# Gathering experts' tokens from unscaled rows, and a fourth staged piece of weights in the tile this frees

## The chip, the cores and the metric

The kernel runs on one core of a Trainium2 chip. The metric is the device time of one execution, in microseconds (us). Before the change it is 1026.22 us, the median of three runs (1024.59, 1026.22 and 1026.88 us).

## The reference

Two transformer blocks for 256 tokens of width 1024, all in float32. The change touches the end of the first block, a mixture of experts whose router picks, for each token, one of 4 groups and then 2 of its 8 experts:

```
xf = _rmsnorm(h, norm_g).reshape(t, d)          # h * rsqrt(mean(h*h) + eps) * norm_g
...                                             # group and expert logits, top 2, gates
def expert_block(args):
    xb, e = args                                # rows of xf that chose expert e
    hid = jax.nn.silu(xb @ w_gate[e]) * (xb @ w_up[e])
    return hid @ w_down[e]
...
y = jnp.zeros((t, d), out.dtype).at[token_of].add(out)   # out is scaled by the gate
h = h + y
```

Each of the 32 experts has three matrices of 2 MB (gate, up, down), so that 192 MB are read once. Every number that the experts see is a row of `h` times one factor per row (the rsqrt) times one gain per channel (`norm_g`, called `norm_ffn` in the kernel).

## The kernel before

Before the experts the kernel runs dense layers on TensorE (PE), each block of weights loaded by SyncE's queue (SP), rounded by ScalarE (ACT) and completed by VectorE (DVE). The last two dense blocks are `co1` and `xv2`; `xv2` is computed in quarters, and between them PE computes the router's logits from the turned rows `h2T`.

The experts run in 8 quads of four. For one quad PE first **gathers**: `gather` multiplies the normed rows (`normed`, as the stationary operand, 8 chunks of 128 channels by 2 tiles of tokens) with `sel3`, a matrix of ones and zeros that `select_slots` on DVE makes, so that each of the four experts gets up to 32 columns. ACT (`gathered_low`) and DVE (`gathered_high`) move the result out of PSUM into `xgT`. Then six weight units follow, of four pieces each (one per expert): u = 0 and 1 are the halves of gate, 2 and 3 those of up, 4 and 5 those of down. The first four are consumed in line 2875, the last two in line 2894. `scatter` brings the outputs back to token order, scaled by the gates, and DVE's `add_outputs` adds them to `h`. In the next quad the gather comes before the scatter of the quad before it.

The order of the loads is written out by hand in SP's program. A unit occupies one of four buffers (`weight_unit`), and a load waits until PE has used what lies there: `moe.unit_used` counts used units, `moe.first_used` the first halves of u = 0 and u = 1. For the first quad much is loaded ahead, while the dense layers still run, into tiles that happen to be free. Three of the four pieces of its unit u = 4 (the first half of down) are **staged** in such tiles: piece 0 in part of `main` and `squares`, piece 2 in `y_slots` and `wide_gain`, piece 1 in `mem2T`. When PE has used buffer 0, ACT copies them there (`place_staged`). The fourth piece has no tile and is loaded straight into buffer 0 after PE has used it, in two halves (line 728). Behind it, line 733 loads u = 5 (four pieces, 4 MB) in eight halves into buffer 1, each group of four once PE has used the first or the second half of u = 1. `load_quad` goes on with the second quad.

`wide_gain` holds `norm_ffn` broadcast to all partitions until DVE has normed the rows (`norm_tokens`); only then SP loads the second half of piece 2 into it (line 671). The tile `normed` takes junk of ACT's squares and then the normed rows, and these are read by all 8 gathers. Channels are stored there by chunks (`by_chunk`): the channel 8p + k of a row lies at position 128k + p, since the experts' weights are read with channel 8p + k in partition p.

Of the kernel before, what the change touches and what calls it, by code (L numbers as in the profile page):

```python
# [27 lines left out]
ALU = mybir.AluOpType  # L28
# [3 lines left out]
P = 128  # L32
T = 256
TT = T // P
# [28 lines left out]
EXTRA_PARTS = ((0, 4, 0, 4), (1, 8, 0, 4))  # L63
# [101 lines left out]
SCALED_ROWS = ["h2", "h3"]  # L165
# [52 lines left out]
def build(nc, A, out):  # L218
    with ExitStack() as ctx:
# [21 lines left out]
        def as_f32(x):  # L241
# [23 lines left out]
        wide_gain = sb("wide_gain", [P, D])  # L265
        lam_s = sb("lam_s", [P, 8])
# [111 lines left out]
                  [y_slots, wide_gain[:, :]]]  # L378
# [66 lines left out]
        staged_landed = [sem(f"staged_piece_landed{i}") for i in range(3)]  # L445
# [153 lines left out]
        def _(sp):  # L599
# [23 lines left out]
            for t in range(TT):  # L623
# [4 lines left out]
                      (wide_gain[:, :], A["norm_ffn"].broadcast_to([P, D])),  # L628
# [35 lines left out]
            def load_staged(i, halves=range(2)):  # L664

                if i == 1:
                    whole = mem2T.rearrange("p (k n) -> p k n", k=FC // 2)
                    sp.dma_start(whole, down_w_of[i, :, 0:2, :]).then_inc(staged_landed[i], 16)
                else:
                    for k in halves:  # L670
                        sp.dma_start(staged[i][k], down_w_of[i, :, k, :]).then_inc(staged_landed[i], 16)

            for name in FIRST_BLOCKS[2:]:
# [8 lines left out]
                elif name == "co0":  # L682
# [3 lines left out]
                    load_unit(2, (2,), up_w_of, 0, at=2)  # L686
                    sp.wait_ge(head_summed, len(HEAD_SQUARES))
# [24 lines left out]
            for half in range(2):  # L712
                for q in range(2):
# [116 lines left out]
        def _(act):  # L830
# [338 lines left out]
            square_rows("h2", h, normed, "co")  # L1169
# [54 lines left out]

            act_quad(0, first=True)
            act.wait_ge(params_landed, 16 * N_PARAMS)
# [156 lines left out]
        def _(dve):  # L1383
# [504 lines left out]

            def by_chunk(x):

                return x.rearrange("p (c q) -> p q c", c=KC)

# [5 lines left out]
            def norm_tokens(t):  # L1898

                v.scalar_tensor_tensor(by_chunk(normed[:, t, :]), h[:, t, :].rearrange("p (q c) -> p q c", c=KC),  # L1900
                                       rstd[:, row0 + t:row0 + t + 1],
                                       wide_gain[:, :].rearrange("p (q c) -> p q c", c=KC),
                                       ALU.mult, ALU.mult).then_inc(normed_ready, 1)

            norm_tokens(0)
            split_lo("xv2", [1])
            norm_tokens(1)

# [104 lines left out]
            def gathered_high(S, n):  # L2013
                dve.wait_ge(S.gathered, n + 1)
                v.tensor_copy(xgT[:, 512:1024], bank[1][:, :]).then_inc(S.hi_drained, 1)

            def add_outputs(S, n, between=None):
# [15 lines left out]
            def dve_quad(S, n, following, between=None):  # L2033
# [9 lines left out]
                add_outputs(S, n, between)  # L2043
# [7 lines left out]
            with dve.Fori(0, 2 * LAST_PAIR) as i:  # L2051
# [18 lines left out]
            for p in range(2):  # L2070
                gathered_high(moe, last_quad + p)
# [1176 lines left out]
```

## Time and profile before

| | |
|---|---|
| profiled execution, its own time | 1026.24 us |
| its span in the trace | 1024.5 us |
| median of three runs | 1026.22 us |
| PE busy | 856.6 us (84%) |
| DVE busy | 458.7 us (45%) |
| ACT busy | 332.9 us (32%) |
| read from memory | 293.40 MB, 287 GB/s over the span |

The span is the time between the first and the last recorded instruction; the execution's own time is 1.74 us longer. The page cuts the span into 40 slices of 25.6 us. PE is at nine tenths in the dense parts, and at five to seven tenths from slice 12 to slice 28, where the experts are; there the DMA engines are at nine tenths throughout.

### The profile page before, as it was taken

What the parts mean: (1) busy time and instruction counts of PE and PEld (TensorE: products, weight loads), DVE (VectorE), ACT (ScalarE), POOL (GpSimd) and SP (SyncE); (2) the same over time, 40 slices, a digit from 0 to 9 for tenths busy, and PEclk for the clock granted to TensorE, in tenths of its full rate; (3) what the DMA queues carried; (4) which work ended last, traced back from release to release, by engine and by line L of the source; (5) the groups of instructions that cost most, each with busy time, mean ns of one, the idle gap of its engine ahead of it and who ended that gap; (6) DMA issues with size and microseconds to landing.
All of it is one profiled execution on the core that took longest, in us unless ns stands there. A gap on an engine that the chain in (4) does not pass through costs nothing.

```text
span 1024.5 us, 13523 instructions
## 1 busy us (share of the span) xinstructions
PE 856.6 (84%) x5437; PEld 593.4 (58%) x5437; DVE 458.7 (45%) x859; ACT 332.9 (32%) x534; POOL 23.2 (2%) x35
## 2 busy tenths in 40 slices
PE   8998999999994566767566666656999999999997
PEld 8877888798631131313112131312788899999995
DVE  4778676574621020201102021010876788656695
ACT  5656654764320000000001000000534555455532
POOL 1030010100000000000000000000000000000000
PEclk9999999999998897878869788888999999999999
DMA  9743466587999999999999999999555354444541
GB/s 324 263 165 104 154 230 234 177 335 267 357 402 423 420 422 421 422 421 420 423 421 422 422 421 420 422 421 404 186 189 180 124 165 133 156 151 138 185 143 44
DMA packets 76287, 295.29 MB, mean 288 GB/s; under 512 B 6754, under 2 KB 7236, under 8 KB 53828
## 3 DMA queue, kind: packets, MB, share of 16 engines
q1 hardware_dynamic: 73876, 291.37, 73.9%
q10 hardware_dynamic: 2352, 3.10, 0.9%
q8 instruction: 41, 0.67, 0.3%
q14 instruction: 18, 0.15, 0.0%
HBM read 293.40 MB, written 1.05 MB: 287 GB/s over the span
## 4 chain that ended last, share of the span: by engine, by line
PE 58%; DMA 17%; SPq 14%; DVE 6%; ACT 2%; issue 2%; POOL 0%; POOLq 0%; ACTq 0%; DVEq 0%
DMA ring<-in_w_e_down 16%; PE bank L2448 12%; SPq L644 11%; PE bank L2450 11%; PE bank L2449 11%; PE bank L2894 4%; PE bank L2875 3%; PE bank L2850 3%; SPq L659 2%; PE bank L2382 2%; PE bank L2926 2%; DVE ring_rounded L1445 2%; ACT ring_rounded L907 1%; DMA ring<-in_w_in 1%; PE bank L2979 1%
## 5 line engine op out<-in xcount | busy, mean ns | idle before, releaser
L1445 DVE TENSOR_TENSOR ring_rounded<-ring,ring_rounded 128x2048 fp32r<-128x2048 f32 x79 | 181.0, 2291 | 120.4 <-ACT ring_rounded L907 120.0
L907 ACT ACTIVATE ring_rounded<-ring 128x2048 fp32r<-128x2048 f32 x79 | 151.3, 1915 | 170.3 <-PE bank L2450 157.1
L2875 PE MATMUL bank<-ring,main 128*32 128x512 f32 x768 | 116.6, 762 | 75.1 <-DMA ring<-in_w_e_up 53.4
L2449 PE MATMUL bank<-ring_rounded 128*128 128x256 f32 (+1 forms) x456 | 143.5, 315 | 0.0
L2450 PE MATMUL bank<-ring_rounded 128*128 128x512 f32 x320 | 124.9, 390 | 0.0
L2875 PEld LDWEIGHTS bank<-ring,main 128*32 128x32 f32 x768 | 28.3, 135 | 154.2 <-issue 87.5
L2025 DVE TENSOR_TENSOR h<-bank,h 128x512 f32<-128x512 f32 x32 | 22.0, 690 | 166.0 <-PE bank L2926 166.0
L2894 PE MATMUL bank<-ring,main 128*32 128x512 f32 x384 | 61.0, 789 | 39.9 <-DMA ring<-in_w_e_down 39.2
L2448 PE MATMUL bank<-uT_rounded,ring_rounded 128*128 128x256 f32 x320 | 92.7, 290 | 0.0
L2450 PE MATMUL bank<-uT_rounded,ring_rounded 128*128 128x256 f32 x320 | 90.5, 283 | 0.0
L2449 PEld LDWEIGHTS bank<-ring_rounded 128*128 128x128 f32 x456 | 86.9, 191 | 5.0
L2448 PE MATMUL bank<-ring_rounded,uT_rounded 128*128 128x512 f32 x208 | 82.7, 398 | 1.7 <-ACT main L1265 0.8
L2449 PE MATMUL bank<-ring_rounded,uT_rounded 128*128 128x512 f32 x208 | 81.1, 390 | 0.0
L2010 DVE SCALAR_TENSOR_TENSOR main<-main,bank 128x512 f32<-128x512 f32 x8 | 5.5, 687 | 140.2 <-PE bank L2875 140.2
L2450 PEld LDWEIGHTS bank<-ring_rounded 128*128 128x128 f32 x320 | 60.1, 188 | 12.9
L2894 PEld LDWEIGHTS bank<-ring,main 128*32 128x32 f32 x384 | 14.1, 137 | 83.2 <-DMA ring<-in_w_e_down 48.7
L2448 PEld LDWEIGHTS bank<-uT_rounded,ring_rounded 128*128 128x128 f32 x320 | 61.3, 192 | 1.7 <-issue 1.4
L2450 PEld LDWEIGHTS bank<-uT_rounded,ring_rounded 128*128 128x128 f32 x320 | 61.3, 192 | 0.0
L1188 ACT ACTIVATE main<-bank 128x512 f32<-128x512 f32 x8 | 4.8, 597 | 158.2 <-PE bank L2382 158.2
L2448 PE MATMUL bank<-ring_rounded 128*128 128x512 f32 x136 | 54.2, 398 | 1.5 <-DVE ring_rounded L1431 0.9
L1196 ACT ACTIVATE main<-bank 128x512 f32<-128x512 f32 x16 | 9.6, 597 | 123.5 <-PE bank L2894 123.5
L2448 PEld LDWEIGHTS bank<-ring_rounded,uT_rounded 128*128 128x128 f32 x208 | 39.1, 188 | 11.8 <-issue 2.1
(334 smaller groups left out, 1333.8 us busy)
## 6 DMA issues: line engine op xcount, KB each, us to landing
ring<-in_w_in SPq DMA_DIRECT2D x46, 1024.0 KB, 5.1
ring<-in_w_e_gate SPq DMA_DIRECT2D x44, 1024.0 KB, 25.9
ring<-in_w_e_up SPq DMA_DIRECT2D x44, 1024.0 KB, 26.2
ring<-in_w_e_down SPq DMA_DIRECT2D x36, 1024.0 KB, 25.9
main<-in_w_e_down SPq DMA_DIRECT2D x13, 1024.0 KB, 26.6
main<-in_w_e_up SPq DMA_DIRECT2D x12, 1024.0 KB, 26.9
main<-in_w_e_gate SPq DMA_DIRECT2D x12, 1024.0 KB, 26.4
ring<-in_w_ckv SPq DMA_DIRECT2D x8, 1024.0 KB, 5.0
```

Of the source, the lines that this page charges most:

```text
L644: sp.dma_start(weight_unit(b, at + i, chunks), w_of[e, :, h * n:(h + 1) * n, :])\
L659: sp.dma_start(weight_unit(unit_buffer(p, u), i, chunks)[:, k:k + 1, at], w_of[e, :, 2 + k:3 + k, at]).then_inc(last_landed[n], 16)
L907: a.activation(rounded(hi_half(name, h)), raw_half(name, h), ACT.Copy).then_inc(hi_made, 1)
L1445: v.tensor_tensor(rounded(raw), raw, as_f32(hi_half(name, h)), ALU.subtract).then_inc(split_made, 1)
L2025: v.tensor_tensor(hs, b[:, :], hs, ALU.add).then_inc(S.added, 1)
L2382: return nc.tensor.transpose(dst, src, ident[0:k, 0:k])
L2448: mm(dst, left[0], right[0], start=first, stop=False, skip_group_check=True)
L2449: mm(dst, left[0], right[1], start=False, stop=False, skip_group_check=True)
L2450: last = mm(dst, left[1], right[0], start=False, stop=last_one, skip_group_check=True)
L2850: last = mm(dst, normed[:, t, k * P:(k + 1) * P], sel3[:, t, :], start=t == 0, stop=t == TT - 1)
L2875: last = mm(bank[2 + part][on, :], xg3[:, h * (KC // 2) + k, on], weight_unit(unit_buffer(p, u), e, KC)[:, k, :], start=h + k == 0, stop=h ...
L2894: ins = mm(bank[4 + half][on, :], hidT3[:, c, on], weight_unit(unit_buffer(p, u), e, FC)[:, k, half * 512:half * 512 + 512], start=c == 0, ...
```

## The change

- PE gathers from `h` itself, not from `normed`. The chunk of channels is picked by the access pattern: 128 channels at a distance of 8 floats (32 bytes) instead of 128 adjacent ones. The gather now comes before any sum is added to `h`.
- The row factor goes into the selection: `select_slots` multiplies the ones by `rstd`. The channel gain is applied where `xgT` is filled: ACT's one copy of 512 columns becomes four of 128 with a scale, DVE's copy becomes a multiplication by the broadcast gain. `norm_tokens` is gone, and with it PE's and SP's waits for it. The gain is loaded as 128 x 8 (`expert_gain`) instead of 128 x 1024.
- The experts' sums go to `normed`: the first quad is copied there, quads 1 to 5 are added there, quads 6 and 7 go to `h` as before, and behind the gather of quad 7 DVE adds `normed` to `h` (2 instructions of 128x1024).
- `normed` is thereby free while the first block's last dense layers run, and takes the fourth piece of u = 4. It is loaded with the second half of piece 2 ahead of `load_staged(0)`; both halves of line 728 are gone, and ACT places four pieces. ACT's junk of the squares of `h2` goes to `main` and `xv2`.

```diff
-EXTRA_PARTS = ((0, 4, 0, 4), (1, 8, 0, 4))
+EXTRA_PARTS = ((0, 4, 0, 4), (0, 8, 0, 4))
...
-                  [y_slots, wide_gain[:, :]]]
+                  [y_slots, wide_gain[:, :]], [normed[:, 0, :], normed[:, 1, :]]]
...
-                      (wide_gain[:, :], A["norm_ffn"].broadcast_to([P, D])),
+                      (expert_gain[:, :], A["norm_ffn"][0].rearrange("(p k) -> p k", p=P)),
...
                     load_unit(2, (2,), up_w_of, 0, at=2)
+                    load_staged(3)
+                    load_staged(2, [1])
                     sp.wait_ge(head_summed, len(HEAD_SQUARES))
                     load_staged(0)
...
                         load_unit(2, (GROUP - 1,), up_w_of, 0, at=GROUP - 1)
-                        sp.wait_ge(normed_ready, 2 * SCALED_ROWS.index("h2") + 2)
-                        load_staged(2, [1])
             load_staged(1)
-            for k, used in enumerate((moe.first_used, moe.unit_used)):
-                sp.wait_ge(used, 1)
-                sp.dma_start(weight_unit(0, GROUP - 1, FC)[:, k:k + 1, :], down_w_of[GROUP - 1, :, k:k + 1, :])\
-                    .then_inc(unit_landed[0], 16)
...
-            square_rows("h2", h, normed, "co")
+            for t in range(TT):
+                wait_drained(act, f"co0_{t}")
+                wait_drained(act, f"co1_{t}")
+                at = NORM_AT["h2"][1] + t
+                ins = a.activation((main[:, 0:D], xv2)[t], h[:, t, :], ACT.Square, accum_out=mean_sq[:, at:at + 1])
+            ins.then_inc(row_squared, 1)
...
-                a.activation(xgT[:, 0:512], bank[0][:, :], ACT.Copy).then_inc(S.lo_drained, 1)
+                for k in range(KC // 2):
+                    ins = a.activation(xgT[:, k * P:(k + 1) * P], bank[0][:, k * P:(k + 1) * P], ACT.Copy,
+                                       scale=expert_gain[:, k:k + 1])
+                ins.then_inc(S.lo_drained, 1)
...
-                for i, parts_ in ((0, 2), (2, 2), (1, 1)):
+                for i, parts_ in ((0, 2), (2, 2), (3, 1), (1, 1)):
...
-            norm_tokens(0)
             split_lo("xv2", [1])
-            norm_tokens(1)
...
-                        last = v.tensor_scalar(select[:, lo:lo + CAP], slot_no[:, :], rank_flat[:, col], None,
-                                               ALU.is_equal)
+                        last = v.tensor_scalar(select[:, lo:lo + CAP], slot_no[:, :], rank_flat[:, col],
+                                               rstd[:, row0 + t:row0 + t + 1], ALU.is_equal, ALU.mult)
...
-                        hs = h[:, t, half * 512:half * 512 + 512]
-                        v.tensor_tensor(hs, b[:, :], hs, ALU.add).then_inc(S.added, 1)
+                        at = slice(half * 512, half * 512 + 512)
+                        if into == "new sums":
+                            ins = v.tensor_copy(normed[:, t, at], b[:, :])
+                        else:
+                            to = (normed if into == "sums" else h)[:, t, at]
+                            ins = v.tensor_tensor(to, b[:, :], to, ALU.add)
+                        ins.then_inc(S.added, 1)
...
+            gathered_high(moe, last_quad + 1)
+            dve.wait_ge(moe.added, last_quad * 4 + 8)
+            for t in range(TT):
+                ins = v.tensor_tensor(h[:, t, :], normed[:, t, :], h[:, t, :], ALU.add)
+            link(ins)
...
-                        last = mm(dst, normed[:, t, k * P:(k + 1) * P], sel3[:, t, :], start=t == 0,
-                                  stop=t == TT - 1)
+                        last = mm(dst, h[:, t, :].rearrange("p (q c) -> p c q", c=KC)[:, k, :], sel3[:, t, :],
+                                  start=t == 0, stop=t == TT - 1)
...
-            pe.wait_ge(normed_ready, 2 * SCALED_ROWS.index("h2") + 2)
```

SP's queue, before, around the early loads behind the dense block `co0` (line 616 loads dense blocks, 644 whole pieces of expert units, 671 halves of staged pieces; the semaphore that a load waits for stands in brackets):

```order
L616 DMA ring<-in_w_co 128x4x512 [waits bank_filled1]
L644 DMA ring<-in_w_e_gate 128x2048 [waits bank_filled1]
L644 DMA main<-in_w_e_up 128x2048 [waits row_squared]
L671 DMA main<-in_w_e_down 128x1024 [waits head_summed]
L671 DMA squares<-in_w_e_down 128x1024
L644 DMA main<-in_w_e_up 128x2048 [waits bank_filled7]
L644 DMA ring<-in_w_e_gate 128x2048 [waits bank_filled3]
```

The same place in SP's queue now:

```order
L617 DMA ring<-in_w_co 128x4x512 [waits bank_filled1]
L645 DMA ring<-in_w_e_gate 128x2048 [waits bank_filled1]
L645 DMA main<-in_w_e_up 128x2048 [waits row_squared]
L669 DMA normed<-in_w_e_down 128x2048
L672 DMA wide_gain<-in_w_e_down 128x1024
L672 DMA main<-in_w_e_down 128x1024 [waits head_summed]
L672 DMA squares<-in_w_e_down 128x1024
L645 DMA main<-in_w_e_up 128x2048 [waits bank_filled7]
L645 DMA ring<-in_w_e_gate 128x2048 [waits bank_filled3]
```

Two loads, 1 MB into `normed` and 0.5 MB into `wide_gain`, have moved in here, without a wait of their own.

SP's queue, before, from the last piece that is loaded ahead into the first loads that wait for the first quad (`moe_half_of_first_unit_used` is `moe.first_used`, `moe_weight_unit_used` is `moe.unit_used`):

```order
L668 DMA main<-in_w_e_down 128x2048
L728 DMA ring<-in_w_e_down 128x1024 [waits moe_half_of_first_unit_used]
L728 DMA ring<-in_w_e_down 128x1024 [waits moe_weight_unit_used]
L733 DMA ring<-in_w_e_down 128x1024 [waits moe_half_of_first_unit_used]
L733 DMA ring<-in_w_e_down 128x1024 x3
L733 DMA ring<-in_w_e_down 128x1024 [waits moe_weight_unit_used]
L733 DMA ring<-in_w_e_down 128x1024 x3
L644 DMA main<-in_w_e_gate 128x2048 [waits moe_weight_unit_used]
```

And now:

```order
L669 DMA main<-in_w_e_down 128x2048
L730 DMA ring<-in_w_e_down 128x1024 [waits moe_half_of_first_unit_used]
L730 DMA ring<-in_w_e_down 128x1024 x3
L730 DMA ring<-in_w_e_down 128x1024 [waits moe_weight_unit_used]
L730 DMA ring<-in_w_e_down 128x1024 x3
L645 DMA main<-in_w_e_gate 128x2048 [waits moe_weight_unit_used]
```

The two halves of line 728 are gone, so that nothing stands between the last piece loaded ahead and the eight halves of u = 5, whose first waits as before for the second count of `moe.first_used`.

## Rows read from the trace of the kernel before

**Rows 1.** The page's part 2: what the DMA engines moved, in 40 slices.

```profile
GB/s 324 263 165 104 154 230 234 177 335 267 357 402 423 420 422 421 422 421 420 423 421 422 422 421 420 422 421 404 186 189 180 124 165 133 156 151 138 185 143 44
```

**Rows 2.** Engines by stretch: length, busy us and instructions, PE's clock, DMA share, GB/s.

```profile
203.00:224.00 21.00, 21.00 (x148) 20.00 (x147) 15.74 (x36) 14.86 (x33) 1.31 (x1) 1.00 1.00 397
...
228.00:231.00 3.00, 3.00 (x15) 2.59 (x14) 0.78 (x2) 1.28 (x4) 0.00 (x0) 1.00 0.00 0
...
281.00:285.00 4.00, 4.00 (x40) 1.17 (x36) 0.22 (x1) 3.75 (x6) 0.00 (x0) 1.00 0.89 309
...
540.00:600.00 60.00, 38.63 (x244) 13.34 (x241) 7.83 (x24) 3.96 (x7) 0.00 (x0) 0.86 1.01 421
```

**Rows 3.** Timeline of SP's queue: start, length of issuing, line, what is loaded.

```profile
202.42 0.59 SPq L671 DMA_DIRECT2D main<-in_w_e_down  x1
...
216.04 6.92 SPq L616 DMA_DIRECT2D ring<-in_w_co  x2
...
262.68 0.43 SPq L671 DMA_DIRECT2D wide_gain<-in_w_e_down  x1
...
275.39 2.04 SPq L728 DMA_DIRECT2D ring<-in_w_e_down  x2
279.33 4.86 SPq L733 DMA_DIRECT2D ring<-in_w_e_down  x8
```

**Rows 4.** Loads issued at 216.04, 230.37, 277.10 and 279.33: size, us to landing.

```profile
ring<-in_w_co SPq DMA_DIRECT2D x1, 1024.0 KB, 8.8
...
ring<-in_w_e_gate SPq DMA_DIRECT2D x1, 1024.0 KB, 4.9
...
ring<-in_w_e_down SPq DMA_DIRECT2D x1, 512.0 KB, 5.5
...
ring<-in_w_e_down SPq DMA_DIRECT2D x1, 512.0 KB, 4.6
```

**Rows 5.** Timeline of PE in the first quad: gather, then unit u = 0.

```profile
269.74 3.73 PE L2850 MATMUL bank<-main,normed 128*128 128x128 f32 x32
273.40 3.64 PE L2875 MATMUL bank<-ring,main 128*32 128x512 f32 x32
```

**Rows 6.** Weight loads (ns min/median/max): gather, hidden at 288, probabilities at 224.

```profile
L2850 PEld LDWEIGHTS bank<-main,normed x32: 188/192/193, 269.5 to 273.1; 128*128 128x128 f32 x32
...
L2382 PEld LDWEIGHTS bank<-ident,main x4: 198/209/223, 288.7 to 289.0; 128*128 128x128 f32 x4
...
L2382 PEld LDWEIGHTS bank<-ident,main x4: 140/141/144, 223.9 to 224.3; 128*128 128x128 f32 x4
```

**Rows 7.** Chain of waits, four transposes each: hidden at 288, rotated keys at 804.

```profile
288.66 0.75 PE bank L2382 x4
...
804.82 0.66 PE bank L2382 x4
```

**Rows 8.** Timeline of DVE around the router and the first selection.

```profile
260.24 2.03 DVE L1900 SCALAR_TENSOR_TENSOR normed<-h,rstd,wide_gain 128x1024 f32<-128x1024 f32 x1
262.31 0.42 DVE L1924 SCALAR_TENSOR_TENSOR main<-bank,rstd,b_router 128x36 f32<-128x36 f32 x2
...
267.34 1.26 DVE L1990 TENSOR_SCALAR main<-slot_no,rank 128x32 f32<-128x32 f32 x8
...
270.22 1.74 DVE L1999 TENSOR_SCALAR main<-slot_no,rank,gates 128x32 f32<-128x32 f32 x8
```

**Rows 9.** Timeline of ACT: 128-column copies, split of `co1`, first gather's copy, staged pieces.

```profile
206.94 0.42 ACT L844 ACTIVATE main<-bank 128x128 f32<-128x128 f32 x2
...
235.92 1.92 ACT L907 ACTIVATE ring_rounded<-ring 128x2048 fp32r<-128x2048 f32 x1 [4.88 <-PE bank L2450]
...
271.73 0.60 ACT L1201 ACTIVATE main<-bank 128x512 f32<-128x512 f32 x1 [1.00 <-PE bank L2850]
...
280.10 1.06 ACT L1210 ACTIVATE ring<-main 128x1024 f32<-128x1024 f32 x1 [2.69 <-DMA main<-in_w_e_down]
```

**Rows 10.** Chain of waits at the end of the experts, and DVE in the last quad.

```profile
705.71 12.13 DMA ring<-in_w_in
...
678.84 0.69 DVE L2006 SCALAR_TENSOR_TENSOR main<-main,bank 128x512 f32<-128x512 f32 x1 [10.11 <-ACT main L1184]
```

More of the change, by code:

```diff
@@ L164 @@
 ROW_NORMS = ["x", "mem", "h1", "mem2", "h2", "h3", "final"]
-SCALED_ROWS = ["h2", "h3"]
+SCALED_ROWS = ["h3"]
 HEAD_SQUARES = ["dq0", "dq1", "dk0", "dk1", "og0", "og1", "ck0", "ck1", "ck2", "ck3",
@@ L265, in build @@
         wide_gain = sb("wide_gain", [P, D])
+        expert_gain = sb("expert_gain", [P, KC])
         lam_s = sb("lam_s", [P, 8])
@@ L444, in build @@
         moe = ExpertSems(sem, "moe")
-        staged_landed = [sem(f"staged_piece_landed{i}") for i in range(3)]
+        staged_landed = [sem(f"staged_piece_landed{i}") for i in range(GROUP)]
         last_landed = [sem(f"last_unit_chunk_landed{k}") for k in range(3)]
@@ L664, in load_staged @@
             def load_staged(i, halves=range(2)):
-                if i == 1:
-                    whole = mem2T.rearrange("p (k n) -> p k n", k=FC // 2)
+                if i in (1, 3):
+                    whole = mem2T.rearrange("p (k n) -> p k n", k=FC // 2) if i == 1 else normed[:, :, :]
                     sp.dma_start(whole, down_w_of[i, :, 0:2, :]).then_inc(staged_landed[i], 16)
@@ L1223, in act_quad @@
                 expert_out(moe, n)
+            act.wait_ge(params_landed, 16 * N_PARAMS)
             act_quad(0, first=True)
-            act.wait_ge(params_landed, 16 * N_PARAMS)
             a.activation(rounded(w_ikw_hi), w_ikw[:, :, :].rearrange("p k n -> p (k n)"), ACT.Copy)\
@@ L1886, in _ @@
             add_to_h("co", following=("co1", "xv2"))
-            def by_chunk(x):
-                return x.rearrange("p (c q) -> p q c", c=KC)
             in_order(dve, row_squared, ROW_NORMS, "h2")
@@ L1896, in _ @@
             _, row0, _ = NORM_AT["h2"]
[L1898 to L1903, printed above, removed]
-            norm_tokens(0)
             split_lo("xv2", [1])
-            norm_tokens(1)
             rc = Carver(rt, 0, 512)
@@ L2014, in gathered_high, with add_outputs @@
                 dve.wait_ge(S.gathered, n + 1)
-                v.tensor_copy(xgT[:, 512:1024], bank[1][:, :]).then_inc(S.hi_drained, 1)
-            def add_outputs(S, n, between=None):
+                gain = expert_gain[:, KC // 2:KC].rearrange("p (k o) -> p k o", o=1).broadcast_to([P, KC // 2, P])
+                v.tensor_tensor(xgT[:, 512:1024].rearrange("p (k s) -> p k s", k=KC // 2),
+                                bank[1][:, :].rearrange("p (k s) -> p k s", k=KC // 2), gain, ALU.mult)\
+                    .then_inc(S.hi_drained, 1)
+            def add_outputs(S, n, into, between=None):
                 for half in range(2):
@@ L2031, in shift_ranks, with dve_quad @@
                 v.tensor_scalar(at, at, -float(CAP), None, ALU.add).then_inc(S.ranks_shifted, 1)
-            def dve_quad(S, n, following, between=None):
+            def dve_quad(S, n, following, into="sums", between=None):
                 dve.wait_ge(S.gathered, n + 1)
@@ L2042, in dve_quad @@
                 hidden(S, n)
-                add_outputs(S, n, between)
+                add_outputs(S, n, into, between)
             select_slots(moe, 0)
@@ L2050, in _ @@
             mark(moe.added, 4)
-            with dve.Fori(0, 2 * LAST_PAIR) as i:
+            gathered_high(moe, 0)
+            dve_quad(moe, 0, 1, "new sums")
+            with dve.Fori(1, 2 * LAST_PAIR) as i:
                 gathered_high(moe, i)
@@ L2068, in _ @@
             last_quad = dve.snap(over * (2 * MORE_PAIRS) + 2 * LAST_PAIR)
-            for p in range(2):
-                gathered_high(moe, last_quad + p)
-                dve_quad(moe, last_quad + p, None if p else QUADS - 1,
-                         (lambda: split_lo("iq", [0])) if p else None)
+            gathered_high(moe, last_quad)
+            dve_quad(moe, last_quad, QUADS - 1, "rows")
+            gathered_high(moe, last_quad + 1)
[3 more added lines that the diff above has]
+            link(ins)
+            dve_quad(moe, last_quad + 1, None, "rows", lambda: split_lo("iq", [0]))
             mark(after_experts, 1)
```

## The prediction

> **What bounds the kernel now.** I first read the page's slices: from slice 12 to slice 27 the DMA engines move 420 to 423 GB/s without a dent, and less before and after [rows 1]. The table of stretches says the same of a whole period of two quads: 60 us, DMA share 1.01, 421 GB/s, while PE is busy for 38.63 us [rows 2]. So the experts' stage is a stream of 192 MB at full rate, and PE waits for it. The chain of waits ends the stage with a transfer: the first weights of the second block are issued at 705.71 us behind all expert weights and land 12.13 us later, and all behind them follows [rows 10]. What is saved in the stage is therefore only what makes this stream end earlier: bytes that go earlier into time in which the DMA engines stood still, as long as the stream then has no new hole. Before the stream PE is dense: it is busy for all of 203 to 224 and 228 to 231 us [rows 2], and its gather at 269.74 is followed by u = 0 at 273.40 without a gap [rows 5]. There PE's time sets when buffers come free, and so when loads start.
>
> **The bytes moved.** From behind 262 us go the half piece into `wide_gain` (0.5 MB, issued at 262.68) and the two halves of line 728 (1 MB, the first issued at 275.39, the second behind it at 277.10) [rows 3]. In all 1.5 MB, 1.573 million bytes, at 421 GB/s [rows 2]: 3.7 us. If the engines had no pause on either side, the stream would end 3.7 us earlier.
>
> They now go in at about 202.4 us, ahead of the staged piece 0 [rows 3]. The engines are full there until 224 and move nothing at all from 228 to 231 us [rows 2], and the shift of 3.7 us fits nearly into that pause. What is queued behind: `co1`, first half, issued at 216.04 and landed 8.8 us later, at 224.8 [rows 3, 4]. It would land at 228.6, and ACT takes it at 235.92, having waited for PE, not for it [rows 9]: 7 us of cover. SP's own issuing of two more loads (0.4 to 0.6 us each, [rows 3]) is covered by the wait before 216.04. The moved bytes cost nothing there.
>
> **Where the expected gain is cut.** Line 733 loads u = 5, and its first half waits until PE has used half of u = 1. It was issued at 279.33 and landed 4.6 us later, at 283.9 [rows 3, 4]. It did not land sooner because line 728 was ahead of it: the second half there landed at 277.10 + 5.5 = 282.6 [rows 4]. In the changed kernel nothing moves PE's point in time: gather, u = 0 and u = 1 follow each other on PE [rows 5], and the gather starts when `xv2` is done, not when the rows are normed. The router's logits were read by DVE at 262.31, 0.04 us behind the second `norm_tokens` (260.24 + 2.03) [rows 8], but PE delivered them only then, so dropping the norm gives nothing here either. So the last thing in front of line 733 is piece 1, which landed at 280.1 [rows 9] and, with the 0.5 MB of `wide_gain` gone ahead (1.2 us), lands at 278.9. The queue is then empty when line 733 is issued. A megabyte alone in the queue takes 4.9 us [rows 4]; half a megabyte takes 1.2 us less, 3.7 us, and lands at 283.0 instead of 283.9. The stream runs 0.9 us ahead from there, not 3.7: the other 2.8 us become a pause of the DMA engines between about 277 and 281 us. Even in the kernel before, the engines were down to a share of 0.89 from 281 to 285 us [rows 2], which shows how shallow the queue is at that point. The bounds of this term are 0 (the eight halves are issued over 4.86 us, and the shallow queue takes the lead back) and 3.7 us (something lets line 733 start earlier). I take 0.9, from the landing times. Behind it the loads of the second quad are gated by PE at times that do not change, but the queue is more than 10 us deep by then, so the lead stays to the end.
>
> **The gather.** Its price counts in full once: what the first gather takes longer moves line 733 and the whole stream. In the other quads PE has 21 us to spare in 60 [rows 2]. Before, 32 loads and matmuls took 3.73 us, u = 0 starting 3.66 us behind their start [rows 5]: 0.114 us each. Now the stationary operand is read with a step of 32 bytes. No row shows that step. The nearest is the transpose of the hidden rows, read with a step of 16 bytes: its weight loads take 209 ns against 141 ns for adjacent columns [rows 6], but four of them in a row, both times from a standstill, take 0.75 against 0.66 us [rows 7]. The pitch thus grows by 0.09/4 = 0.022 us, times 32 is 0.7 us. The bounds: nothing (the loads stay hidden behind the matmuls), and twice the pitch, 3.7 us. In between lies 32 x (209 - 141) ns = 2.2 us, if the longer load showed fully. I take 0.7 us, the nearest row.
>
> The Trainium skill, "SBUF — State Buffer", section "Door 1: The DMA port swizzle", states that memory is read in lines of 16 bytes, that at least two accesses must fall into a line to hide the access, and that four fp32 of step are free; eight are not. The trace agrees at four only roughly (+0.09 us in four) and has nothing at eight. By the rule the gather pays more than the 0.7 us; how much it does not say.
>
> **The rest, all at nothing.** `select_slots` gets a second operation; its eight instructions cost like `select_gates`, 1.74 instead of 1.26 us [rows 8], and end at 269.1, before PE's gather at 269.74 [rows 5]: 0.6 us of cover, beyond which each us would count. ACT's four copies of 128 columns: two take 0.42 us [rows 9], so four some 0.75 to 0.84 us instead of 0.60; they start at 271.73 and have until u = 0 at 273.40. DVE's copy of the other half becomes a multiplication of the same shape, needed only by u = 1. ACT places a fourth piece, twice 1.06 us more, but no longer waits 2.69 us for piece 1 in the middle [rows 9]. The two additions of 128x1024 in the last quad stand before DVE's step at 678.84, before which DVE was idle for 10.11 us [rows 10]. The smaller gain load at the start shortens a queue on which PE does not wait.
>
> **Sum.** Against the profiled execution's own 1026.24 us (span 1024.5, and 1.74 around it; the median is 1026.22, the same): -0.9 + 0.7 = -0.2, so 1026.0 us.
>
> **Rivals.**
> - *The step of 32 bytes doubles the weight load.* PE's pitch goes from 0.114 to about 0.23 us and the first gather lasts 3.7 us longer; line 733 starts at 283 instead of 279.33, with nothing to fill the pause. For it: the load of the 16-byte step is already longer by half [rows 6]. Against it: hardly any of that shows in the pitch [rows 7]. Time: 1026.24 - 0.9 + 3.7 = 1029.0 us. It decides from 0.028 us more per load on (0.9/32); slower by over 0.2% from 0.092 us. This is also the side on which the skill's rule stands.
> - *The whole 3.7 us arrive.* It needs the DMA engines to have no pause before line 733, that is a backlog of over 3 us at 279.33 in which line 728 was only a part. For it: shares near 1 up to there and a page that shows the stage full. Against it: the landing at 283.9, only 4.6 us after the issue [rows 4]. Time: 1026.24 - 3.7 + 0.7 = 1023.2 us.
> - *The early bytes collide.* If the pause at 228 to 231 us did not take them, `xv2` and the partial pieces would come late on a dense PE. Cover is 7 us, so I price it at 1 to 3 us with little chance: about 1028 us.
>
> **How the numbers follow.** About 0.2% (2 us) is what a measurement of this kernel can tell from no change. Forecast (lead 0 to 2 us, gather 0 to 2 us): 55%. Doubled load: 20%. Full gain: 20%. Collision or another loss: 5%. The forecast's own range is 1024.2 to 1028.2, and nearly all of it within 0.2%, with some at either edge. So faster by over 0.2%: 0.20 from the full gain and 0.04 from the forecast; slower: 0.16 of the doubled load, 0.03 of the collision and 0.03 of the forecast; same 0.54. The range is 1022.8 to 1029.2: it takes in both large rivals and leaves out their tails.
>
> **What would show it.** Right: the first gather at the same start and 3.7 to 4.5 us long; the first half of u = 5 issued within 1 us of 279.33, landing some 3.7 us later; DMA engines nearly still between 278 and 281 us; the second block's first weights landing at about 717.6. Wrong: a gather of 5 us or more, with u = 5 issued later by as much; or no pause before 281 us and an end 3 us earlier; or ACT's split of `co1` waiting for a transfer at 236 us; or the selection later than PE's gather.

## The result: slower by 0.28%, and the profile after

| | before | changed |
|---|---|---|
| median | 1026.30 us (9 runs) | 1029.02 us (9 runs) |
| lowest, highest | 1024.59, 1027.62 us | 1028.56, 1031.06 us |
| profiled execution, span | 1026.24, 1024.5 us | 1029.58, 1027.8 us |

The ratio is 1.0028, with a 95% interval of 1.0019 to 1.0037: the kernel became slower, where no change (1026.0 us) was forecast. The time lies inside the range given (up to 1029.2), but on the side of a rival, the one in which the weight loads of the gather double (1029.0 us, 20%).

The timeline of PE in the first quad of the changed kernel, gather and then u = 0, answers to [rows 5]:

```profile
269.80 7.66 PE L2854 MATMUL bank<-main,h 128*128 128x128 f32 x32
277.39 3.64 PE L2879 MATMUL bank<-ring,main 128*32 128x512 f32 x32
```

The gather starts within 0.06 us of where it started before, but takes 7.66 instead of 3.73 us. Its weight loads, of all gathers, answer to the first line of [rows 6]:

```profile
L2854 PEld LDWEIGHTS bank<-main,h x256: 312/335/338, 269.6 to 671.7; 128*128 128x128 f32 x128
```

335 ns where there were 192, and one load per 7.59/32 = 0.237 us instead of 0.114. The queue of SP from the last early piece on answers to [rows 3]:

```profile
270.92 0.43 SPq L669 DMA_DIRECT2D main<-in_w_e_down  x1
283.31 4.42 SPq L730 DMA_DIRECT2D ring<-in_w_e_down  x8
```

Nothing is issued for 12 us; the eight halves of u = 5 start at 283.31 instead of 279.33. What the DMA engines did meanwhile stands in the last two columns of the table by stretches:

```profile
276.00:278.00 2.00, 2.00 (x15) 1.55 (x18) 0.50 (x1) 0.00 (x0) 0.00 (x0) 1.00 0.66 277
278.00:281.00 3.00, 3.00 (x33) 0.69 (x21) 1.84 (x9) 1.62 (x2) 0.00 (x0) 1.00 0.01 5
281.00:284.00 3.00, 3.00 (x34) 1.04 (x34) 1.91 (x9) 3.00 (x5) 0.00 (x0) 1.00 0.00 0
```

The two later of these stretches in the kernel before:

```profile
278.00:281.00 3.00, 3.00 (x32) 0.91 (x28) 1.49 (x8) 0.90 (x1) 0.00 (x0) 1.00 1.00 362
281.00:284.00 3.00, 3.00 (x32) 0.91 (x28) 0.00 (x0) 3.00 (x5) 0.00 (x0) 1.00 0.83 311
```

The DMA engines now stand still for over six microseconds, from about 277.5 to beyond 284, while PE is fully busy: a hole in the stream that nothing fills later. The early bytes, in contrast, went where they were expected to go. The same table earlier, against the second line of [rows 2]:

```profile
224.00:228.00 4.00, 4.00 (x24) 3.52 (x23) 3.77 (x4) 2.95 (x7) 0.00 (x0) 1.00 1.04 386
228.00:231.00 3.00, 3.00 (x15) 2.62 (x14) 0.98 (x2) 1.08 (x4) 0.00 (x0) 1.00 0.57 207
```

The pause at 228 to 231 us, empty before, now carries 207 GB/s, and `co1` is not late. ACT's split of it, against [rows 9], still waits for PE:

```profile
236.10 1.92 ACT L904 ACTIVATE ring_rounded<-ring 128x2048 fp32r<-128x2048 f32 x1 [4.87 <-PE bank L2454]
```

The stream of weights itself is unchanged at full rate, and its end, in the chain of waits, answers to the first line of [rows 10]:

```profile
708.86 12.00 DMA ring<-in_w_in
...
720.88 1.91 ACT ring_rounded L904
```

The second block's first weights land at 720.86 us, 3.0 us later than before (717.84, from 705.71 + 12.13 in [rows 10]), and all behind them is later by about that.

### The profile page after: what moved, and what is told of

It is laid out like the page before. It is cut to its first block, busy times and chain, and to the rows that moved or that the text cites. A ratio compares the mean times of both kernels' runs of the same rounds, so it can differ in the third digit from the quotient of the medians.

```text
span 1027.8 us, 13523 instructions
## 1 busy us (share of the span) xinstructions
PE 879.5 (86%) x5437; PEld 625.2 (61%) x5437; DVE 461.3 (45%) x859; ACT 339.3 (33%) x560; POOL 23.2 (2%) x35
## 4 chain that ended last, share of the span: by engine, by line
PE 65%; DMA 17%; SPq 7%; DVE 5%; ACT 2%; issue 2%; ACTq 0%; POOL 0%; POOLq 0%; DVEq 0%
DMA ring<-in_w_e_down 16%; PE bank L2452 12%; PE bank L2454 11%; PE bank L2453 11%; PE bank L2854 6%; PE bank L2879 6%; SPq L645 5%; PE bank L2898 4%; PE bank L2386 3%; SPq L660 2%; PE bank L2930 2%; DVE ring_rounded L1450 2%; ACT ring_rounded L904 1%; DMA ring<-in_w_in 1%; PE bank L2982 1%
## 5 line engine op out<-in xcount | busy, mean ns | idle before, releaser
L2879 PE MATMUL bank<-ring,main 128*32 128x512 f32 x768 | 109.3, 721 | 56.3 <-DMA ring<-in_w_e_up 55.0
L2898 PE MATMUL bank<-ring,main 128*32 128x512 f32 x384 | 62.9, 812 | 42.6 <-DMA ring<-in_w_e_down 41.8
L2022 DVE TENSOR_TENSOR normed<-bank,normed 128x512 f32<-128x512 f32 x20 | 13.8, 692 | 120.3 <-PE bank L2930 120.3
L2854 PEld LDWEIGHTS bank<-main,h 128*128 128x128 f32 x256 | 61.7, 334 | 9.6 <-issue 9.3
L2854 PE MATMUL bank<-main,h 128*128 128x128 f32 x256 | 62.4, 405 | 4.4 <-issue 4.4
L1190 ACT ACTIVATE main<-bank 128x512 f32<-128x512 f32 x8 | 4.8, 597 | 153.7 <-PE bank L2386 153.7
```

Of the source, the lines that this page charges most:

```text
L2854: last = mm(dst, h[:, t, :].rearrange("p (q c) -> p c q", c=KC)[:, k, :], sel3[:, t, :], start=t == 0, stop=t == TT - 1)
L2879: last = mm(bank[2 + part][on, :], xg3[:, h * (KC // 2) + k, on], weight_unit(unit_buffer(p, u), e, KC)[:, k, :], start=h + k == 0, stop=h ...
L2898: ins = mm(bank[4 + half][on, :], hidT3[:, c, on], weight_unit(unit_buffer(p, u), e, FC)[:, k, half * 512:half * 512 + 512], start=c == 0, ...
```

## The experiments

Each experiment is an edit of the changed kernel, or of the kernel before where this is said. A ratio is that to the kernel before, run again beside the experiment. Where a number is an end of the stream, it is the start of ACT's first instruction behind the landing of the second block's first weights, 717.86 us before and 720.88 us after; it is read from one profiled execution, while the times are medians. The experiments `e1_adjacent`, `e2_adjacent_first_only`, `e3_before_step8` and `e9_adjacent_swap` do the same work but give the experts their channels in another order than their weights have, so their results are not those of the reference; `e4_steps` and `e10_operands` compute other things in the first gather, ran once each, and only their traces are used.

**Adjacent channels in the gather.**

```diff
-    last = mm(dst, h[:, t, :].rearrange("p (q c) -> p c q", c=KC)[:, k, :], sel3[:, t, :],
+    last = mm(dst, h[:, t, k * P:(k + 1) * P], sel3[:, t, :],
```

> The changed kernel, but the gather takes 128 adjacent channels instead of 128 at a step of 32 bytes (so the experts see the channels in another order; nothing else is left out). Theory (the step doubles the weight load of the first gather, and that moves the whole stream): gather back from 7.66 to 3.7 us, u = 5 issued at 279.4 us, time 1026.3 - 0.9 = about 1025.4 us. Rival (the loss comes from the rest of the change, the early bytes, the gains or the additions): the gather shrinks but the time stays near 1029.0.

1024.83 us, ratio to before 0.9990 (0.9982 to 0.9999). PE, SP and the stretch from 278 to 281 us in this kernel:

```profile
269.70 3.73 PE L2854 MATMUL bank<-main,h 128*128 128x128 f32 x32
279.29 4.10 SPq L730 DMA_DIRECT2D ring<-in_w_e_down  x8
...
278.00:281.00 3.00, 3.00 (x32) 0.91 (x28) 1.33 (x7) 2.92 (x5) 0.00 (x0) 1.00 0.16 27
```

The gather is back to 3.73 us, and the issue of u = 5 to 279.29. The rival is out: the early bytes, the gains, the fourth placed piece and the additions cost nothing that shows. The stream ends at 715.98 us, 1.9 us ahead of the kernel before, although a short pause of the DMA engines is left in front of u = 5 (the last line above).

**Adjacent channels in the first quad's gather only.**

```diff
-    gather(moe, of_quad(j, 0, 1, 0))
+    gather(moe, of_quad(j, 0, 1, 0), isinstance(j, int) and j == 0)
```

> As e1_adjacent, but only the gather of the first quad takes adjacent channels; the other seven keep the step of 32 bytes (the experts of the first quad see another channel order). Theory (only the first gather is on the path, the others hide behind the stream of weights): the same time as e1_adjacent, about 1025.4 us. Rival (the seven other gathers, 3.9 us longer each, also count, for example by freeing buffers later): near 1028 us.

1025.36 us, ratio 0.9992 (0.9983 to 1.0001). The end of the stream is 716.08 us, 0.1 us from that with all gathers fast. The other seven slow gathers, in a stage in which PE waits for the stream, cost nothing that these runs can tell (the medians are 0.5 us apart, each kernel's own runs 2.6 to 2.8 us).

**The kernel before, with the step of 32 bytes.**

```diff
-    last = mm(dst, normed[:, t, k * P:(k + 1) * P], sel3[:, t, :], start=t == 0,
+    last = mm(dst, normed[:, t, :].rearrange("p (q c) -> p c q", c=KC)[:, k, :], sel3[:, t, :], start=t == 0,
```

> The kernel before, with only the gather's access pattern of the change: 128 channels of the normed rows at a step of 32 bytes (so the channels are permuted a second time and the experts see them in another order). Theory: all 32 loads of a gather at 0.235 us, the first gather 7.66 us, and line 728 and 733 issued 3.9 us later; after the last early bytes land near 280 us the DMA engines pause, so 1026.3 + 3.9 - up to 0.5 = 1029.7 to 1030.2 us, and the changed kernel's 1029.0 is this minus the 0.9 us of the moved bytes. Rival (unscaled rows or the moved bytes are what costs): 1026.3 us.

1030.61 us, ratio 1.0042 (1.0029 to 1.0055), a gather of 7.68 us, the eight halves issued at 283.52 and the stream ended at 722.50 us. The pattern alone makes the kernel before slower by more than the whole change does. The changed kernel is 1.6 us ahead of it, in the median as at the end of the stream (1030.61 - 1029.02, 722.50 - 720.88): that is what the rest of the change, the moved bytes above all, is worth beside a slow gather. The time expected was up to 1030.2 us, with 0.9 us for the moved bytes: both came out somewhat larger.

**Eight steps in one gather.**

```diff
+    flat = h[:, :, :].rearrange("p t d -> p (t d)")
+    if k == 3:      # one such line for each k, with c = 1, 2, 3, 4, 5, 6, 8, 16
+        last = mm(dst, flat[:, 0:512].rearrange("p (q c) -> p c q", c=4)[:, 0, :], sel3[:, t, :], **more)
```

> The changed kernel with a different step in each of the gather's eight chunks: 1, 2, 3, 4, 5, 6, 8 and 16 floats (4, 8, 12, 16, 20, 24, 32 and 64 bytes), four loads each, each on a line of its own (the experts get wrong channels). Theory (a line of 16 bytes must be hit twice): 0.114 us per load up to 8 bytes, more from 12 or 16 bytes on, the same from 16 bytes as at 32, 0.235 us. Rival (the cost sets in only beyond 16 bytes, as the four transposes at 16 bytes suggested): 0.12 to 0.14 us at 16 bytes, 0.235 us at 20 bytes and more. Second rival (it grows with the step): 64 bytes dearer than 32.

The timeline of PE, one line for each step in that order, and then the first line of u = 0:

```profile
270.39 0.60 PE L2857 MATMUL bank<-main,h 128*128 128x128 f32 x4
270.83 0.64 PE L2859 MATMUL bank<-main,h 128*128 128x128 f32 x4
271.30 0.86 PE L2861 MATMUL bank<-main,h 128*128 128x128 f32 x4
272.00 1.09 PE L2863 MATMUL bank<-main,h 128*128 128x128 f32 x4
272.93 1.06 PE L2865 MATMUL bank<-main,h 128*128 128x128 f32 x4
273.83 1.06 PE L2867 MATMUL bank<-main,h 128*128 128x128 f32 x4
274.73 1.11 PE L2869 MATMUL bank<-main,h 128*128 128x128 f32 x4
275.68 1.04 PE L2871 MATMUL bank<-main,h 128*128 128x128 f32 x4
276.65 1.92 PE L2895 MATMUL bank<-ring,main 128*32 128x512 f32 x16
```

To be read by the starts: from one line to the next are 0.44, 0.47, 0.70, 0.93, 0.90, 0.90, 0.95 and 0.97 us for four loads. So 4 and 8 bytes of step cost 0.11 to 0.12 us per load, 12 bytes 0.175, and from 16 bytes on it is 0.23 to 0.24 whatever the step. Both rivals are out: the cost is there at 16 bytes already, as large as at 32, and it does not grow up to 64. With them goes the estimate of the prediction.

**Transposes, and the rows as the moving operand.**

```diff
+    if k == 1:      # k = 0 to 3: c = 1, 4, 8, 16, two transposes for each t
+        transpose(dst, flat[:, 0:512].rearrange("p (q c) -> p c q", c=4)[:, 0, :])
+    if k == 6:      # k = 4 to 7: c = 1, 2, 4, 8
+        last = mm(dst, sel3[:, t, :], flat[:, 0:512].rearrange("p (q c) -> p c q", c=4)[:, 0, :], **more)
```

> The changed kernel with other work in the gather's eight chunks (the experts get wrong numbers): four transposes each at a step of 1, 4, 8 and 16 floats, and then two products each with the selection as the loaded operand and the rows as the moving one, at 1, 2, 4 and 8 floats. Theory (a transpose hides the step, since only one of its two loads, or none, pays): transposes at 16 bytes near 0.12 us each and the same at 32, so that the row of before could not have told the gather's price. Rival (transposes at 32 bytes double as the gather does, and 16 bytes is the last cheap step for them): 0.12 us at 16 bytes, 0.23 us at 32 bytes. For the moving operand: either no price up to 32 bytes, or the same doubling as for the loaded one.

```profile
269.81 1.98 PE L2386 MATMUL bank<-ident,h 128*128 128x128 f32 x16
271.63 0.61 PE L2869 MATMUL bank<-h,main 128*128 128x128 f32 x4
272.07 0.62 PE L2871 MATMUL bank<-h,main 128*128 128x128 f32 x4
272.53 1.06 PE L2873 MATMUL bank<-h,main 128*128 128x128 f32 x4
273.42 1.11 PE L2875 MATMUL bank<-h,main 128*128 128x128 f32 x4
```

The first line holds the sixteen transposes, the others four products each, at steps of 4, 8, 16 and 32 bytes. Sixteen transposes at four different steps take 1.82 us up to the next start, 0.114 us each, the pitch of adjacent columns. So a transpose's pitch does not grow with its step; why it does not is not settled by this. Their weight loads do get longer in the record, 138 to 139 ns at 4 bytes and 191 to 211 ns at 16 bytes and more, while the pitch stays. The rows from which the prediction took the gather's price, transposes at 16 bytes [rows 6, 7], could not have shown it. A moving operand pays as the loaded one does: 0.44 and 0.46 us for four at 4 and 8 bytes, 0.89 at 16, and 1.04 at 32 (up to 274.46, where u = 0 starts).

**A step of 8 bytes for all quads.** All computation is kept; the channels are divided so that partition p holds channels 256g + 2p and 256g + 2p + 1.

```diff
-    gate_w_of = A["w_e_gate"][0].rearrange("e (p k) n -> e p k n", p=P)      # up likewise, and the gains
+    gate_w_of = A["w_e_gate"][0].rearrange("e (g p k) n -> e p g k n", g=4, p=P)
...
+    last = mm(dst, h[:, t, :].rearrange("p (g q c) -> p g c q", g=4, c=2)[:, k // 2, k % 2, :], sel3[:, t, :],
```

> The changed kernel with all of its computation, but the channels are divided so that a gather reads at a step of 8 bytes: channel 256g + 2p + k in partition p, in the loads of gate and up, in the gains and in the gather. Theory (the step decides, and 8 bytes cost 0.117 us per load as in the sweep of steps): first gather 3.8 us, time as with adjacent channels, 1024.8 to 1025.4 us. Rival (the shorter runs in memory, 4 KB instead of 8 KB, cost the stream of weights its rate): 421 GB/s falls, and at 1% the time is 4 us longer, about 1029 us.

1033.83 us, ratio 1.0078 (1.0065 to 1.0091): the rival, and more of it than the 1029 us that it was priced at. The gather did take only 3.92 us and the eight halves went out at 279.45, but the stream is slower for good. The same stretch in the kernel before moved at 421 GB/s [rows 2]:

```profile
540.00:600.00 60.00, 36.46 (x242) 13.03 (x236) 8.31 (x24) 3.91 (x9) 0.00 (x0) 0.87 1.02 414
```

That is 1.7% less, at a share of busy DMA engines of 1.02 against 1.01, and over the 440 us of the stage some 7 us, more than the gather's 3.9. The same trace says which loads are slow. Only gate and up have the runs of 4 KB; the third matrix, down, keeps its 8 KB. From 360 to 390 us nearly all packets are under 8 KB (3176 of 3177) and the rate is 409 GB/s. From 395 to 410 us, where the pieces of down arrive, it is 422 GB/s (279 packets of 1231 are under 8 KB from 392 to 412 us). So the loads with runs of 4 KB lose 3%, and those with 8 KB nothing. Whether the run in memory or the smaller packet costs it, these runs do not tell apart.

**A step of 16 bytes for all quads,** the same edit with g = 2 and c = 4, which keeps runs of 8 KB.

> As e5_step2, but with channel 512g + 4p + k in partition p: a step of 16 bytes, and runs of 8 KB as in the changed kernel. Theory (16 bytes cost as much as 32, as the sweep of steps showed; runs of 8 KB keep the rate): first gather 7.6 us, stream at 421 GB/s, 1029 us. Rival (four floats of step are free): gather 3.8 us and 1025 us. Second rival (what slowed e5_step2 was not the length of the runs but the division of the channels): stream at 414 GB/s and over 1035 us.

1028.51 us, ratio 1.0024 (1.0015 to 1.0033), a gather of 7.50 us, the stream at 422 GB/s. The division of the channels costs nothing that shows, the length of the runs is what `e5_step2` paid for, and four floats of step are not free.

**The halves swapped.** The staged pieces are those of u = 5 and are placed in buffer 1; the eight halves that wait are those of u = 4 and go to buffer 0, which PE has used a unit earlier. ACT therefore copies the staged pieces a unit later, behind its work on the gates. Part of the edit:

```diff
                 for k, used in enumerate((moe.first_used, moe.unit_used)):
-                sp.wait_ge(used, 2)
+                sp.wait_ge(used, 1)
                 for e in range(GROUP):
-                    sp.dma_start(weight_unit(1, e, FC)[:, k:k + 1, :], down_w_of[e, :, 2 + k:3 + k, :])\
-                        .then_inc(unit_landed[1], 16)
+                    sp.dma_start(weight_unit(0, e, FC)[:, k:k + 1, :], down_w_of[e, :, k:k + 1, :])\
+                        .then_inc(unit_landed[0], 16)
...
-                    ins = a.activation(weight_unit(0, i, FC)[:, k, :], staged[i][k], ACT.Copy)
+                    ins = a.activation(weight_unit(1, i, FC)[:, k, :], staged[i][k], ACT.Copy)
```

> The changed kernel, step of 32 bytes kept, but the staged pieces are those of u = 5 and go to buffer 1, and the eight halves that wait for the first quad are those of u = 4 and go to buffer 0, which PE has used one unit (3.94 us) earlier. Theory (the loss is when these eight halves are issued, and the pause of the DMA engines before them): issued at 279.4 instead of 283.3 us, pause back to that of e1_adjacent, so the slow gather is made up for: about 1024.8 to 1025.5 us. Rival (the slow gather costs PE's time itself, not the issue): stays near 1029 us.

1025.17 us, ratio 0.9989 (0.9980 to 0.9997), with the slow gather still in place:

```profile
272.19 7.66 PE L2854 MATMUL bank<-main,h 128*128 128x128 f32 x32
...
281.76 4.09 SPq L730 DMA_DIRECT2D ring<-in_w_e_down  x8
```

This profiled execution was some 2.4 us late before the gather began, so the distance counts: 9.6 us from the gather to the issue, against 13.5 in the changed kernel and 9.6 before. The swap gives back 3.85 us of the median without making PE any faster. PE reaches u = 0 as late as in the changed kernel, yet with the loads issued at the distance of `e1_adjacent` the time is that of `e1_adjacent` within 0.4 us. So what the slow gather costs the kernel is the point at which the next loads are issued. It still costs that here: with the swap and adjacent channels (`e9_adjacent_swap` below) the loads go out 4 us earlier again, and the time is 3.1 us shorter.

**Both, with a step of 8 bytes for all quads.** The two edits above together.

> Both: the step of 8 bytes of e5_step2 and the swapped halves of e6_swap, all computation kept. Theory: the eight halves are issued at 275.3 us, before piece 1 has landed at about 278.9, so the DMA engines have no pause and the whole 3.7 us of the moved bytes arrive: 1022.0 to 1022.8 us. Rival (the lead is given back later, or u = 4 lands too late for PE at 290 us): 1024 to 1025 us.

1030.46 us, ratio 1.0041 (1.0028 to 1.0054). The number expected is missed, since it took the rate of the stream as given: it runs at 413 and 414 GB/s over 60 us, as in `e5_step2`. Against that kernel the swap is worth 3.4 us, and the engines now move 396 GB/s from 278 to 281 us.

**Both, with adjacent channels.**

> The kernel of e6_swap with the gather of e1_adjacent (adjacent channels, so the experts see another channel order). Theory (the moved bytes are worth 3.7 us of stream, of which e1_adjacent lost some 2 us in the pause before u = 5): no pause, first weights of the second block landing 3.7 to 4.3 us before those of the kernel before, 1022.2 to 1022.8 us. Rival (1024.8 us is all that the moved bytes give): 1024.5 to 1025.5 us.

1022.04 us, ratio 0.9962 (0.9950 to 0.9974), the stream ended at 712.74 us, 5.1 us before that of the kernel before, where 3.7 to 4.3 were expected; the medians are 3.9 us apart (1025.98 beside it). Once nothing makes a hole behind them, the moved bytes bring the whole of the 3.7 us worked out for them. The bytes of the two traces tell where most of the rest arises: from 262 to 290 us this kernel moves 10.51 MB and the kernel before 10.09 MB, so that with the 1.57 MB moved ahead it is 1.99 MB in front, 4.7 us at 421 GB/s. Between 279 and 290 us the kernel before had a shallow queue and did not use its DMA engines fully (309 GB/s from 281 to 285 us [rows 2]).

**The step of 8 bytes in the first quad alone, without and with the swap.** Both keep all computation. Only the loads of the first quad's gate and up are divided as in `e5_step2`, with a second tile of gains.

```diff
+    gate_first = A["w_e_gate"][0].rearrange("e (g p k) n -> e p g k n", g=4, p=P)
...
-    load_unit(0, (0,), gate_w_of, 0)        # and all loads of the first quad likewise
+    load_unit(0, (0,), gate_first, 0)
...
+    last = mm(dst, (h[:, t, :].rearrange("p (g q c) -> p g c q", g=4, c=2)[:, k // 2, k % 2, :] if first else
...
```

> As e11_first_step2_swap, but with the halves not swapped. Theory: the pause of the DMA engines is back and the time is that of e1_adjacent, 1024.6 to 1025.4 us. Rival (the swap only matters beside a slow gather): the same as e11_first_step2_swap.

1024.36 us, ratio 0.9985 (0.9976 to 0.9994), with the pause back:

```profile
278.00:281.00 3.00, 3.00 (x36) 0.91 (x32) 1.47 (x8) 2.81 (x5) 0.00 (x0) 1.00 0.17 22
```

> All computation kept: the swapped halves of e6_swap, and the channel division of e5_step2 (step of 8 bytes, runs of 4 KB in memory) for the first quad alone, with a gain tile of its own; the other seven quads keep the step of 32 bytes and runs of 8 KB. Theory (the first gather alone is on the path, the rate of the stream suffers only where the runs are short): gather 3.9 us, stream at 421 GB/s, 1022.3 to 1023.3 us. Rival (the early loads with short runs are slower by 2% of 16 MB or collide with the dense layers): 1024 us and more.

1021.56 us, ratio 0.9956 (0.9944 to 0.9968), 4.4 us better than the kernel before (1025.98 us beside it) and 7.5 us better than the changed one. It is the lowest median of all, though not clear of the 1022.04 us of `e9_adjacent_swap`, and a little lower than expected. PE, SP and the stretches in it:

```profile
269.78 3.92 PE L2870 MATMUL bank<-main,h 128*128 128x128 f32 x32
...
275.62 3.95 SPq L746 DMA_DIRECT2D ring<-in_w_e_down  x8
...
278.00:281.00 3.00, 3.00 (x32) 0.91 (x28) 1.60 (x8) 1.50 (x3) 0.00 (x0) 1.00 1.02 401
540.00:600.00 60.00, 41.34 (x223) 12.84 (x223) 11.83 (x29) 2.77 (x5) 0.00 (x0) 0.80 1.01 422
```

The hole is gone, the rate is kept, and the stream ends at 712.18 us.

Taken together, where the bytes are moved and the stream keeps its rate, the times follow the point of issue. Eight halves issued at 283.3 to 283.5 us give 1029.02 and 1028.51 us, at 279.3 to 279.4 us they give 1024.83, 1025.36 and 1024.36 (and 1025.17 with the swap beside the slow gather), at 275.4 to 275.6 us 1022.04 and 1021.56. The first 4 us of issuing later cost 2.8 us and the next 4 us cost 4.2: until about 277 us the DMA engines still have other loads to move.

## Why the prediction was wrong

**What bounds the kernel, and where the moved bytes go: right.** The stage ends with the stream, and a change counts only by when the stream ends. The early bytes filled the pause at 228 us. `co1` was expected to land at 228.6 and landed 12.7 us behind its issue at 216.16, at 228.9, 7 us before ACT took it. The kernel with adjacent channels shows in one piece that nothing else of the change costs anything.

**Where the gain is cut: right in kind, too small in size.** The pause in front of u = 5 came as described (0.16 of the engines from 278 to 281 us in the kernel with adjacent channels), and filling it brought the gain back. But the term was 0.9 us, and the lead is 1.6 us in the median (1026.46 us beside it, minus 1024.83) and 1.9 us at the end of the stream with a fast gather, and 1.6 us beside a slow one. The 0.9 came from the landing of the first half alone, and there it was right. From 262 to 284 us the kernel with adjacent channels moves 6.67 MB and the kernel before 7.86, so with the 1.57 MB moved ahead it leads by 0.38 MB, 0.9 us. By 290 us (9.16 against 10.09 MB) it leads by 0.64 MB, 1.5 us. The prediction feared that the shallow queue would take the lead back; it was the kernel before that lost time to its own shallow queue, with 386 GB/s from 285 to 290 us against 415. The last 0.4 us up to the end of the stream are not accounted for.

**The gather: the step that failed.** The prediction set it at 0.7 us, "the nearest row", four transposes at a step of 16 bytes. It was 3.93 us (7.66 - 3.73), a little beyond the upper bound of 3.7. Two runs show why. In the sweep of steps 16 bytes are already as dear as 32, so the row did not lie short of the rise in cost but behind it; and the pitch of transposes does not grow with the step at all, so it could not have shown the rise. The 0.09 us between the two groups of transposes, from which the 0.7 us came, tell nothing of the gather. Nor was the row beside it, a weight load of 209 against 141 ns [rows 6], a measure: among the sixteen transposes the loads grow by as much and the pitch stays, and the gather before, with adjacent channels, already had loads of 192 ns. The nearest row was near in its step and not in its kind of instruction.

**That the gather's price counts once and in full: right, with its mechanism now shown.** The seven later gathers cost nothing that shows, and the first one costs by the point of issue that it moves, as the swap shows. The price is a little more than the gather's own 3.93 us: 4.2 us between the medians with and without the step (1029.02 and 1024.83; in the kernel before 1030.61 and 1026.46), and 4.9 us between the two ends of the stream. Where the part beyond 3.93 us arises stays open. (One reading on the way was wrong without harm: the 60 us of [rows 2] are the period of one quad, not of two, since a quad is 25.2 million bytes; PE has its 21 us to spare in each quad.)

The doubled load was priced at 1029.0 us, and 1029.02 us were measured. That it fits so closely is luck: the gather was priced at 3.7 us where it costs 4.2, and the lead at 0.9 us where it is 1.6, and the two errors nearly cancel (1026.3 - 1.6 + 4.2 = 1028.9). The forecast failed by the gather's term: with the measured 3.9 for 0.7 its own sum gives 1026.2 - 0.9 + 3.9 = 1029.2 us. With the chance of 20% that the rival had, the mistake is also one of weight: the step had never been seen in the trace and the rule that the prediction cites spoke for a price, and against the rival stood only the pitch of a different instruction.

The Trainium skill, "SBUF — State Buffer", section "Door 1: The DMA port swizzle", states that two hits in a line of 16 bytes are needed to hide the access. The sweep agrees in its steps: with 8 bytes, two columns lie in each 16 bytes, and a load costs 0.12 us; with 12 bytes half of the columns share a line with another, and it costs 0.175; with 16 bytes none does, and it costs 0.23. The transposes do not follow it, at least not in their pitch. The skill's figure that four fp32 of step are free is refuted by the sweep for loaded and moving operands: two are nearly free.

**The rest at nothing: right.** The kernel with adjacent channels carries all of it and shows no cost. The first selection took 1.75 us and ended at 269.2, before the gather; ACT's four copies took 1.14 us instead of the 0.75 to 0.84 estimated, still before u = 0; the two additions (2.35 us) stood at 676.93, in a stretch in which DVE waits.

## What to carry to other kernels

When a stage is a stream of transfers, what an engine does in front of it is priced by when it lets the next load go, not by its own time: find the first load that waits for that engine, see what is still in the queue at that moment, and let the load wait for something earlier, as the swapped halves do. Before an operand is read at a step, price that read with an instruction of the same kind; a transposed or otherwise different instruction at the same step tells nothing. And of two ways to lay out data, check the one for the engine against the one for the transfers: the step of 8 bytes won 3.7 us in the one gather that counts and lost more than twice that in the stream (it ended at 724.39 us with the step in all quads and at 716.20 with the step in the first), until it was confined to the one quad in which the gather is on the path.

## What the runs showed of the hardware

- Reading 128 fp32 columns at a step costs PE, per load and at a granted clock of 1.00, 0.11 us at 4 bytes, 0.12 at 8, 0.175 at 12 and 0.23 to 0.24 from 16 to 64 bytes. The moving operand behaves alike (0.11, 0.12, 0.22 and 0.26 us at 4, 8, 16 and 32 bytes), transposes do not (0.114 us over 4, 16, 32 and 64 bytes), though their recorded weight loads grow from 139 to between 191 and 211 ns.
- Loads of 1 MB with runs of 4 KB in memory ran at 409 GB/s where those with runs of 8 KB ran at 421 to 422, in the same kernel (`e5_step2`) and between kernels, with the DMA engines busy throughout in either.
- A half megabyte issued into an empty queue landed after 3.9 us (adjacent channels) and 4.2 us (the changed kernel), where the prediction had worked out 3.7.
